# A hybrid mLSTM and retention step on one core: V of token chunk 1 for both heads in one product of 512 columns

## The chip, the core and the metric

The kernel runs on one NeuronCore of a Trainium2 chip. TensorE multiplies matrices out of SBUF into PSUM, ScalarE and VectorE read PSUM and SBUF and write SBUF, GpSimd (POOL) and SyncE help with elementwise work and issue DMAs. Each engine runs its own queue in order, and they wait for each other on semaphores. The metric is the device time of one execution in microseconds. The kernel before takes 1973.84 us (median of 3 runs, 1972.89 to 1973.92).

## The reference, cut to what matters

Two layers work on 128 context tokens and 512 latent tokens, D = 1024: layer 0 is a bidirectional mLSTM with 4 heads, layer 1 bidirectional retention with 8 heads. Each is followed by a gated feed-forward network. The part that this case is about is the projection of the tokens `u` into V, 256 columns a head:

```
def retention_mixer(u, w_in, decay_exp, g_norm, w_out, S0, grid):
    z = jnp.einsum('btd,de->bte', u, w_in).astype(F32)
    q, k, v, gate = jnp.split(z, [hk, 2 * hk, 2 * hk + hv], axis=-1)
    ...
    v = v.reshape(B, T, B_HEADS, B_DV).transpose(0, 2, 1, 3)
    ...
    h_f, S_f = retention_scan(q, k, v, log_gamma[0], S0[:, 0])
    h_b, S_b = retention_scan(flip_t(q), flip_t(k), flip_t(v), log_gamma[1], S0[:, 1])
```

The mLSTM mixer takes its q, k, v and output gate from `u @ w_in` in the same way. All is float32.

## The kernel before, in words

The 640 tokens are five chunks of 128 (`CH` = 5). Heads are worked on in pairs: two pairs in the mLSTM layer, four in the retention layer, the middle two of those in a hardware loop. For a pair, TensorE makes q, then K (two products each), then V, then for each head scores, gates, states and outputs.

Precision comes from splitting. A weight unit of 128 x 2048 numbers lands by DMA in one of four ring slots. ScalarE rounds it into `w_high[slot % 2]` (`high_unit`, L827), VectorE subtracts and gets the rest into `ring_low[slot]` (`low_unit`, L1388), and a product is the sum of three: high by high, high by low, low by high. There are only two `w_high` buffers for four slots: slot 0 (q, later gates) and slot 2 (V of the pair's first head) share the one, slot 1 (K, later gates) and slot 3 (V of the second head) the other. `high_unit(s, before)` therefore waits until the data has landed and until all products of the unit before in that buffer are made. TensorE waits in `split_unit(slot)` for VectorE's subtraction of that slot (`l_split`).

V is made chunk by chunk by `value_tile` (L2176), 24 matmuls a product (8 steps over D by 3 parts), with the tokens as the stationary operand and the weights streaming. With the weights of one head the product has 256 columns; with both (`w_high_both`, `low_both`) it has 512, one bank of PSUM. Before: chunks 0 and 1 of the first head alone, then `split_unit(3)`, chunks 2 to 4 of both heads, then chunks 0 and 1 of the second head into two banks of one slot. Two PSUM slots alternate (`pj_slot`), and ScalarE copies each product out (L975 and, for the last slot, L980). It starts the split of slot 3 before the V copies (`high_unit(3, 1)`), and that of slot 0, the gate weights, behind the copy of chunk 4 (`high_unit(0, 2)`), since w_high[0] is in use until then.

In the first pair of all, sixteen steps of a modulation product (`between(n)`, L1991, called through `after`) stand between these products. Each uses a row block of `ada_w` that is loaded two steps ahead: the DMA for step n waits for step n−2.

After V, an mLSTM pair has broadcasts of gate rows (L2282, L2283) and then the gate product (L2012); a retention pair has the scores (L2211, L2214) and then the gate product (L2012), which waits in `split_unit(0)`.

Of the kernel before, what the change touches and what calls it, by code (L numbers as in the profile page):

```python
# [9 lines left out]
ACT = mybir.ActivationFunctionType  # L10
# [10 lines left out]
CH = TOK // P  # L21
# [6 lines left out]
DK, DV = 128, 256  # L28
# [46 lines left out]
def hybrid_step(nc, x_prompt, x_sample, st_C, st_n, st_m, st_S, c_lat, c_ctx, norm_gain, ada_w, ada_b,  # L75
# [3 lines left out]
    with ExitStack() as ctx:  # L79
# [38 lines left out]
        w_high = [w_high_both[:, s, :] for s in range(2)]  # L118

        ring, ring_low = [], []  # L120
# [21 lines left out]
        vt = xflat[:, 0:vt_n].rearrange("p (c h v) -> p c h v", c=CH, h=2)  # L142
# [583 lines left out]
        def _(a):  # L726
# [208 lines left out]
            for layer in range(DEPTH):  # L935
# [13 lines left out]
                def evac_qkv(first=False, after=None, led=False):  # L949
                    if first:  # L950

                        a.wait_ge(turned, turnn.add())
                    for t in range(4):
                        out = qk[:, t, :].rearrange("p (b t) -> p b t", b=2)
                        if led and t >= 2:
                            a.wait_ge(made[1], outs[1].add())
                            a.activation(out, lead_more[t - 2], ACT.Copy, scale=DK ** -0.5).then_inc(led_out, 1)
                        else:
                            s = pj(t // 2)
                            a.activation(out, PJ[:, s, :, 0:HALF], ACT.Copy, scale=1.0 if t < 2 else DK ** -0.5  # L960
                                         ).then_inc(pj_free[s], 1)
                        if t == 1:
                            high_unit(2, 0)
                            if first:
                                gate_rows()
                    high_unit(3, 1)

                    a.wait_ge(x_saved, 16 * (layer + 1))
                    for c in range(CH):
                        s = pj(2)  # L970
                        if c < 2:
                            out, src = vt[:, c, 0, 0:DV], PJ[:, s, 0, 0:DV]
                        else:
                            out, src = vt[:, c, :, 0:DV], PJ[:, s, 0, :].rearrange("p (h v) -> p h v", h=2)
                        a.activation(out, src, ACT.Copy).then_inc(pj_free[s], 1)  # L975
                        if first and c == 2:
                            ada_row_out(P_EARLY[0])
                    high_unit(0, 2)
                    s = pj(3)
                    a.activation(vt[:, 0:2, 1, 0:DV], PJ[:, s, :, 0:DV], ACT.Copy).then_inc(pj_free[s], 1)  # L980
                    if first:
                        ada_row_out(P_EARLY[1])
                    if after:
                        after()
# [892 lines left out]
        def _(pe):  # L1877
# [13 lines left out]
            def pj_slot():  # L1891

                s = pjn.n % 2
                pjn.add()
                pe.wait_ge(pj_free[s], free[s].now())
                free[s].add()
                return s
# [212 lines left out]
            for layer in range(DEPTH):  # L2110
# [60 lines left out]
                def value_tile(out, c, high, low):  # L2171

                    for k in range(KT):
                        at = slice(k * DV, (k + 1) * DV)
                        for n, (x, w) in enumerate(((u_high, high), (u_high, low), (u_low, high))):
                            ins = pe.matmul(out, x[:, k, c * P:(c + 1) * P], w[:, :, at] if w is w_high_both or w is low_both else w[:, at],  # L2176
                                            start=(k == 0 and n == 0), stop=(k == KT - 1 and n == 2))
                    return ins

                def kv(after=None, led=False):  # L2180
                    if not led:
                        split_unit(1)
                        for m in range(2):
                            project_unit(1, m)
                            if after:
                                after(2 + m)
                    split_unit(2)
                    for c in range(2):
                        s = pj_slot()
                        value_tile(PJ[:, s, 0, 0:DV], c, w_high[0], ring_low[2]).then_inc(made[2], 1)  # L2190
                        if after:
                            after(4 + c)
                    split_unit(3)
                    for c in range(2, CH):
                        s = pj_slot()
                        value_tile(PJ[:, s, 0, :], c, w_high_both, low_both).then_inc(made[2], 1)
                        if after:
                            after(2 + 2 * c)
                            after(3 + 2 * c)
                    s = pj_slot()  # L2200
                    for c in range(2):
                        ins = value_tile(PJ[:, s, c, 0:DV], c, w_high[1], ring_low[3])
                        if c == 1:
                            ins.then_inc(made[3], 1)
                        if after:
                            after(12 + c)

                def scores(hh):

# [408 lines left out]
```

## Time and profile before

| | |
|---|---|
| median of 3 runs | 1973.84 us |
| profiled execution, own time | 1973.65 us |
| its span | 1971.9 us |
| VectorE busy | 52% |
| ScalarE busy | 35% |
| GpSimd busy | 10% |
| V products (L2176) | 1008 matmuls: 576 of 256 columns, 432 of 512 |

The page's times are of one execution, in microseconds from the span's start. PE is the stream of matmuls, PEld the loading of stationary operands beside it. Matmuls overlap, so what one costs is read from the distance between starts, or from a window over a whole product divided by its count, and not from the duration in its own row. Idle time in brackets at the end of a row of the timeline is that of the engine just before the row, with what ended it.

### The profile page before, as it was taken

The page shows a single profiled execution, that of the slowest core. Times are in us where ns is not written, and L with a number is a line of the kernel's source. Part 1 is how long each engine was busy: PE and PEld are TensorE (multiplying, and loading weights), DVE is VectorE, ACT ScalarE, POOL GpSimd, SP SyncE. Part 2 cuts the span into 40 slices and gives each one's busy share as a digit, 9 for nine tenths or more (in the row PEclk, how much of TensorE's full clock was granted, in tenths as well). Part 3 has the DMA queues.
Part 4 walks back from the last instruction along what each step waited for, and adds up shares of the span by engine and source line. Part 5 has one row for each costly group of instructions (what it writes and reads, how often), then busy time and mean ns, then how long its engine had stood idle before and what let it go on. Part 6 is the DMA issues. An engine that isn't in the chain of part 4 may idle for free.

```text
span 1971.9 us, 30380 instructions
## 1 busy us (share of the span) xinstructions
PE 1911.3 (97%) x12365; PEld 1781.4 (90%) x12365; DVE 1022.0 (52%) x1807; ACT 681.0 (35%) x872; POOL 199.5 (10%) x172
## 2 busy tenths in 40 slices
PE   7989999989999999999999999999999999999998
PEld 5758987759999999998999999998898999999997
DVE  4415446476553555568543343436377664456546
ACT  4314233344331333345322222234344332233333
POOL 4101001410000000141000000001340000000031
PEclk8989999999999999999999999999999999999999
DMA  9851202762213231344232321326742322322153
GB/s 278 315 184 61 90 28 78 256 221 65 77 54 92 76 85 51 94 139 157 70 102 70 102 64 60 111 80 215 229 107 65 86 61 67 104 67 83 34 147 116
DMA packets 270925, 218.84 MB, mean 111 GB/s; under 512 B 7995, under 2 KB 260659, under 8 KB 265203
## 3 DMA queue, kind: packets, MB, share of 16 engines
q1 hardware_dynamic: 261619, 198.96, 33.5%
q10 hardware_dynamic: 7504, 10.74, 1.6%
q0 software_dynamic: 1712, 7.88, 1.1%
q8 instruction: 64, 1.05, 0.2%
q14 instruction: 26, 0.21, 0.0%
HBM read 202.34 MB, written 11.01 MB: 108 GB/s over the span
## 4 chain that ended last, share of the span: by engine, by line
PE 83%; DVE 9%; ACT 2%; DMA 2%; issue 2%; POOL 1%; SPq 0%; DVEq 0%; ACTq 0%; POOLq 0%
PE PJ L2012 47%; PE PJ L2023 10%; PE PJ L2176 8%; PE PJ L2147 2%; PE AT L2033 2%; DVE uT L1311 1%; PE AT L2357 1%; DMA hT<-in_ada_w 1%; PE AT L1991 1%; PE AT L2373 1%; PE PJ L2033 1%; PE PJ L2493 1%; DVE diag L1298 1%; DVE xT L1307 1%; PE AT L2370 1%
## 5 line engine op out<-in xcount | busy, mean ns | idle before, releaser
L2012 PE MATMUL PJ<-h_both,w_high 128*128 128x320 f32 x3616 | 682.5, 311 | 0.3 <-DVE sq L1789 0.3
L2012 PEld LDWEIGHTS PJ<-h_both,w_high 128*128 128x128 f32 x3616 | 569.0, 188 | 3.5 <-issue 2.0
L1789 DVE SCALAR_TENSOR_TENSOR sq<-PJ,cols,sq 128x127 f32<-128x127 f32 (+2 forms) x504 | 189.0, 431 | 239.3 <-ACT sq L1153 228.2
L2012 PE MATMUL PJ<-h_both,w_low 128*128 128x320 f32 x1280 | 291.5, 309 | 0.0
L810 ACT ACTIVATE w_high<-ring 128x2048 fp32r<-128x2048 f32 (+2 forms) x92 | 159.3, 1732 | 166.4 <-PE PJ L2012 103.2
L1374 DVE TENSOR_TENSOR w_low<-ring,w_high 128x2048 fp32r<-128x2048 f32 (+2 forms) x92 | 190.9, 2075 | 45.3 <-ACT w_high L810 45.2
L2012 PEld LDWEIGHTS PJ<-h_both,w_low 128*128 128x128 f32 x1280 | 214.1, 188 | 0.0
L597 POOL TENSOR_TENSOR sqsum<-sqsum,sq 128x320 f32<-128x320 f32 x56 | 106.3, 1899 | 962.5 <-issue 804.8
L2176 PE MATMUL PJ<-w_high,h_both 128*128 128x256 f32 (+1 forms) x672 | 160.5, 330 | 0.0
L1388 DVE TENSOR_TENSOR ring_low<-ring,w_high 128x2048 fp32r<-128x2048 f32 x38 | 86.9, 2286 | 125.7 <-ACT w_high L827 124.6
L1153 ACT ACTIVATE sq<-PJ,cols 128x640 f32<-128x640 f32 x84 | 74.3, 885 | 191.7 <-PE PJ L2012 188.9
L2176 PEld LDWEIGHTS PJ<-w_high,h_both 128*128 128x128 f32 x672 | 114.5, 190 | 16.5 <-issue 5.2
L2012 PE MATMUL PJ<-h_both,ring_low 128*128 128x320 f32 x528 | 121.1, 311 | 0.0
L2176 PE MATMUL PJ<-ring_low,h_both 128*128 128x256 f32 (+1 forms) x336 | 110.4, 329 | 0.0
L2023 PE MATMUL PJ<-act_high,w_high 128*128 128x320 f32 x336 | 105.9, 315 | 1.9 <-DVE w_low L1374 1.8
L2023 PE MATMUL PJ<-act_high,w_low 128*128 128x320 f32 x336 | 103.8, 309 | 0.0
L2023 PE MATMUL PJ<-act_low,w_high 128*128 128x320 f32 x336 | 103.8, 309 | 0.0
L2012 PEld LDWEIGHTS PJ<-h_both,ring_low 128*128 128x128 f32 x528 | 89.0, 189 | 0.0
L2023 PE MATMUL PJ<-h_both,ring_low 128*128 128x320 f32 x288 | 89.0, 309 | 0.0
L2023 PE MATMUL PJ<-h_both,w_high 128*128 128x320 f32 x224 | 71.4, 319 | 2.6 <-DVE ring_low L1382 2.6
L2012 PE MATMUL PJ<-act_high,w_high 128*128 128x320 f32 x320 | 73.0, 309 | 0.0
L2012 PE MATMUL PJ<-act_low,w_high 128*128 128x320 f32 x320 | 72.9, 309 | 0.0
(288 smaller groups left out, 3037.5 us busy)
## 6 DMA issues: line engine op xcount, KB each, us to landing
ring<-in_ffn_w_up SPq DMA_DIRECT2D x88, 512.0 KB, 5.0
hT<-in_ada_w SPq DMA_DIRECT2D x30, 1024.0 KB, 5.5
ring<-in_ret_w_in SPq DMA_DIRECT2D x24, 1024.0 KB, 7.7
ring<-in_ffn_w_down SPq DMA_DIRECT2D x56, 384.0 KB, 4.1
ring<-in_ret_w_out SPq DMA_DIRECT2D x14, 1024.0 KB, 5.9
ring<-in_ml_w_in SPq DMA_DIRECT2D x12, 1024.0 KB, 9.8
turn<-in_ada_w SPq DMA_DIRECT2D x10, 1024.0 KB, 7.4
ring<-in_ffn_w_down SPq DMA_DIRECT2D x32, 320.0 KB, 3.7
```

The costliest lines, as they stand in the source:

```text
L597: pool.tensor_tensor(sum_half[:, b, :], sum_half[:, b, :], sq_y[:, n % 2, :], ALU.add).then_inc(sqy_added, 1)
L810: a.activation(w_high[s][:, 0:wide], ring[s][:, 0:wide], ACT.Copy).then_inc(h_split[s], 1)
L1153: a.activation(conv[:, b, :].rearrange("p (b t) -> p b t", b=2), src, ACT.Identity, scale=cols[:, ds(t + (COL_CONV + (layer * 3 + 1) * 2 * ...
L1298: link(v.reciprocal(rstd_half[:, b, :], rstd_half[:, b, :]))
L1374: v.tensor_tensor(w_low[s][:, 0:wide], ring[s][:, 0:wide], w_high[s][:, 0:wide].bitcast(F32), ALU.subtract).then_inc(l_split[s], 1)
L1388: v.tensor_tensor(ring_low[s][:, :], ring[s][:, :], w_high[s % 2][:, :].bitcast(F32), ALU.subtract).then_inc(l_split[s % 2], 1)
L1789: ins = v.scalar_tensor_tensor(o, z, scalar, o, ALU.mult, ALU.add)
L2012: ins = pe.matmul(PJ[:, s, b, 0:HALF], w[:, at + k * step:at + k * step + P], x[:, k, b * HALF:(b + 1) * HALF], start=(k == 0 and n == 0), ...
L2023: ins = pe.matmul(PJ[:, s, b, 0:HALF], w[:, at + k * step:at + k * step + P], x[:, k, b * HALF:(b + 1) * HALF], start=(k == 0 and n == 0), ...
L2033: ins = pe.matmul(out, w[:, at:at + P], x[:, k, b * HALF:(b + 1) * HALF], start=(k == 0 and n == 0), stop=(k == KT - 1 and n == 2))
L2147: ins = pe.matmul(PJ[:, s, b, 0:HALF], w[:, k * 256 + m * P:k * 256 + (m + 1) * P], x[:, k, b * HALF:(b + 1) * HALF], start=(k == 0 and n ...
L2176: ins = pe.matmul(out, x[:, k, c * P:(c + 1) * P], w[:, :, at] if w is w_high_both or w is low_both else w[:, at], start=(k == 0 and n == ...
```

## The change

Chunk 1 moves from the narrow products to the wide ones, for all six pairs. The first head alone is done for chunk 0 only, then `split_unit(3)` follows, then chunks 1 to 4 for both heads, then chunk 0 of the second head. ScalarE's copies follow the new shapes. The calls of `after` for the first pair are shared out anew: steps 5 and 6 behind chunk 1, 7 and 8 behind chunk 2, 9 and 10 behind chunk 3, 11 and 12 behind chunk 4, 13 behind the last product.

```
--- before.py
+++ after.py
@@ -968,7 +968,7 @@
                     for c in range(CH):
                         s = pj(2)
-                        if c < 2:
+                        if c < 1:
                             out, src = vt[:, c, 0, 0:DV], PJ[:, s, 0, 0:DV]
                         else:
                             out, src = vt[:, c, :, 0:DV], PJ[:, s, 0, :].rearrange("p (h v) -> p h v", h=2)
@@ -977,7 +977,7 @@
                     high_unit(0, 2)
                     s = pj(3)
-                    a.activation(vt[:, 0:2, 1, 0:DV], PJ[:, s, :, 0:DV], ACT.Copy).then_inc(pj_free[s], 1)
+                    a.activation(vt[:, 0, 1, 0:DV], PJ[:, s, 0, 0:DV], ACT.Copy).then_inc(pj_free[s], 1)
@@ -2185,25 +2185,22 @@
                     split_unit(2)
-                    for c in range(2):
+                    for c in range(1):
                         s = pj_slot()
                         value_tile(PJ[:, s, 0, 0:DV], c, w_high[0], ring_low[2]).then_inc(made[2], 1)
                         if after:
                             after(4 + c)
                     split_unit(3)
-                    for c in range(2, CH):
+                    for c in range(1, CH):
                         s = pj_slot()
                         value_tile(PJ[:, s, 0, :], c, w_high_both, low_both).then_inc(made[2], 1)
                         if after:
-                            after(2 + 2 * c)
                             after(3 + 2 * c)
+                            after(4 + 2 * c)
                     s = pj_slot()
-                    for c in range(2):
-                        ins = value_tile(PJ[:, s, c, 0:DV], c, w_high[1], ring_low[3])
-                        if c == 1:
-                            ins.then_inc(made[3], 1)
-                        if after:
-                            after(12 + c)
+                    value_tile(PJ[:, s, 0, 0:DV], 0, w_high[1], ring_low[3]).then_inc(made[3], 1)
+                    if after:
+                        after(13)
```

TensorE's queue in the second mLSTM pair, from the first V product to the gate product, before the change. Only each product's first row is shown; `l_split1` is the wait for VectorE's subtraction of slot 3 and `l_split0` that of slot 2 or 0, `pj_free` the wait for ScalarE's copy.

```order
L2176 MATMUL PJ<-w_high,h_both 128x256 [waits pj_free0,l_split0]
...
L2176 MATMUL PJ<-w_high,h_both 128x256 [waits pj_free1]
...
L2176 MATMUL PJ<-w_high,h_both 128x512 [waits pj_free0,l_split1]
...
L2176 MATMUL PJ<-w_high,h_both 128x512 [waits pj_free1]
...
L2176 MATMUL PJ<-w_high,h_both 128x512 [waits pj_free0]
...
L2176 MATMUL PJ<-w_high,h_both 128x256 [waits pj_free1]
...
L2282 MATMUL AT<-rM,hT 128x512 [waits h_ready]
...
L2012 MATMUL PJ<-h_both,w_high 128x320 [waits pj_free0,l_split0]
```

The same stretch with the change (the lines behind L2176 count three less):

```order
L2176 MATMUL PJ<-w_high,h_both 128x256 [waits pj_free0,l_split0]
...
L2176 MATMUL PJ<-w_high,h_both 128x512 [waits pj_free1,l_split1]
...
L2176 MATMUL PJ<-w_high,h_both 128x512 [waits pj_free0]
...
L2176 MATMUL PJ<-w_high,h_both 128x512 [waits pj_free1]
...
L2176 MATMUL PJ<-w_high,h_both 128x512 [waits pj_free0]
...
L2176 MATMUL PJ<-w_high,h_both 128x256 [waits pj_free1]
...
L2279 MATMUL AT<-rM,hT 128x512 [waits h_ready]
...
L2012 MATMUL PJ<-h_both,w_high 128x320 [waits pj_free0,l_split0]
```

The wait for `l_split1` has moved ahead by one product, and between the last wide product and the wait for `l_split0` there is one narrow product where there were two.

TensorE's queue in the very first pair, from the second V product on, before the change (L1991 is a modulation step, `early_full` its DMA):

```order
L1991 MATMUL AT<-hT,silu_c 2x512 [waits early_full0]
...
L2176 MATMUL PJ<-w_high,h_both 128x256 [waits pj_free1]
...
L1991 MATMUL AT<-hT,silu_c 2x512 [waits early_full1]
...
L2176 MATMUL PJ<-w_high,h_both 128x512 [waits pj_free0,l_split1]
...
L1991 MATMUL AT<-hT,silu_c 2x512 [waits early_full0]
...
L1991 MATMUL AT<-hT,silu_c 2x512 [waits early_full1]
```

And with the change:

```order
L1991 MATMUL AT<-hT,silu_c 2x512 [waits early_full0]
...
L2176 MATMUL PJ<-w_high,h_both 128x512 [waits pj_free1,l_split1]
...
L1991 MATMUL AT<-hT,silu_c 2x512 [waits early_full1]
...
L1991 MATMUL AT<-hT,silu_c 2x512 [waits early_full0]
...
L2176 MATMUL PJ<-w_high,h_both 128x512 [waits pj_free0]
```

Steps 5 and 6 now stand together behind chunk 1, where one product stood between them.

## Rows read from the trace of the kernel before

**Rows 1.** The page, busy time, share and instructions of each engine.
```profile
PE 1911.3 (97%) x12365; PEld 1781.4 (90%) x12365; DVE 1022.0 (52%) x1807; ACT 681.0 (35%) x872; POOL 199.5 (10%) x172
```

**Rows 2.** Windows, L2176 only: stretch, length, busy time, clock, DMA share, GB/s.
```profile
1048.52:1054.28 5.76, 5.76 (x49) 5.76 (x49) 1.00 0.60 139
1054.28:1070.62 16.34, 16.34 (x74) 13.52 (x73) 1.00 0.48 146
1070.62:1076.38 5.76, 5.76 (x49) 5.70 (x47) 1.00 0.00 0
```

**Rows 3.** Timeline, ScalarE, second retention pair: start, us, engine, line, operation.
```profile
1049.32 1.90 ACT L827 ACTIVATE w_high<-ring 128x2048 fp32r<-128x2048 f32 x1
```

**Rows 4.** Timeline, VectorE, the same stretch.
```profile
1051.26 2.29 DVE L1388 TENSOR_TENSOR ring_low<-ring,w_high 128x2048 fp32r<-128x2048 f32 x1 [12.64 <-ACT w_high L827]
```

**Rows 5.** Timeline, ScalarE, VectorE and TensorE around the gate product.
```profile
1071.32 1.91 ACT L827 ACTIVATE w_high<-ring 128x2048 fp32r<-128x2048 f32 x1
...
1073.26 2.29 DVE L1388 TENSOR_TENSOR ring_low<-ring,w_high 128x2048 fp32r<-128x2048 f32 x1 [9.81 <-ACT w_high L827]
...
1077.95 0.69 PE L2012 MATMUL PJ<-h_both,w_high 128*128 128x320 f32 x3
```

**Rows 6.** Windows, all engines: PE, PEld, DVE, ACT, POOL, clock, DMA, GB/s.
```profile
344.70:348.10 3.40, 3.40 (x8) 2.15 (x7) 3.40 (x4) 2.93 (x4) 0.00 (x0) 0.50 0.97 331
348.20:419.70 71.50, 67.27 (x440) 54.33 (x438) 41.05 (x72) 28.70 (x63) 28.54 (x23) 1.00 0.74 256
419.80:423.20 3.40, 3.34 (x9) 1.23 (x12) 3.40 (x9) 1.55 (x4) 0.00 (x0) 0.50 0.00 0
423.30:1960.00 1536.70, 1516.32 (x10010) 1462.05 (x10002) 814.19 (x1320) 527.54 (x601) 128.03 (x82) 1.00 0.32 95
```

**Rows 7.** Timeline, VectorE and TensorE, second mLSTM pair.
```profile
238.23 2.29 DVE L1388 TENSOR_TENSOR ring_low<-ring,w_high 128x2048 fp32r<-128x2048 f32 x1 [12.64 <-ACT w_high L827]
...
241.13 0.52 PE L2176 MATMUL PJ<-w_high,h_both 128*128 128x256 f32 x2
```

**Rows 8.** Timeline, TensorE, the gate product of that pair.
```profile
265.80 0.41 PE L2012 MATMUL PJ<-h_both,w_high 128*128 128x320 f32 x1
```

**Rows 9.** Timeline, VectorE and TensorE, first pair: slot 3's subtraction, modulation steps.
```profile
85.98 2.29 DVE L1388 TENSOR_TENSOR ring_low<-ring,w_high 128x2048 fp32r<-128x2048 f32 x1
...
98.93 0.61 PE L1991 MATMUL AT<-hT,silu_c 128*2 128x512 f32 x4 [1.23 <-DMA hT<-in_ada_w]
...
122.02 0.61 PE L1991 MATMUL AT<-hT,silu_c 128*2 128x512 f32 x4 [1.05 <-DMA hT<-in_ada_w]
...
126.05 0.61 PE L1991 MATMUL AT<-hT,silu_c 128*2 128x512 f32 x4
...
128.09 0.61 PE L1991 MATMUL AT<-hT,silu_c 128*2 128x512 f32 x4 [1.00 <-DMA hT<-in_ada_w]
...
132.09 0.61 PE L1991 MATMUL AT<-hT,silu_c 128*2 128x512 f32 x4 [2.96 <-DMA hT<-in_ada_w]
```

**Rows 10.** Timeline, TensorE: the other idle times of 1.8 to 2.6 us.
```profile
343.98 0.54 PE L2236 MATMUL PJ<-hT,ring 128*128 128x320 f32 x1 [2.32 <-DVE hT L1560]
...
355.59 0.41 PE L2023 MATMUL PJ<-h_both,hT_low 128*128 128x320 f32 x1 [1.82 <-ACT uT L1107]
...
419.12 0.54 PE L1936 MATMUL AT<-sq,common 128*128 128x320 f32 x1 [1.79 <-ACT sq L757]
...
434.58 0.61 PE L1991 MATMUL AT<-hT,silu_c 128*2 128x512 f32 x4 [2.17 <-DMA hT<-in_ada_w]
...
1342.99 0.48 PE L2370 MATMUL AT<-xT,diag 128*128 128x256 f32 x1 [2.56 <-DVE Sst L1692]
```

**Rows 11.** Windows, L2012 only: two gate products of 48 matmuls.
```profile
141.63:150.92 9.29, 9.29 (x48) 9.29 (x48) 0.72 0.00 0
265.80:272.86 7.06, 7.06 (x48) 7.03 (x48) 1.00 0.00 0
```

## The prediction

> **What bounds the kernel now.** I read first the table of engines: TensorE is busy for 97% of the span [rows 1], VectorE for half of it, ScalarE for a third. So the time is TensorE's stream, plus whatever TensorE waits for. Then the windows of the value products (L2176) in the second head pair of the retention layer [rows 2]. Two products of 256 columns take 5.76 us, 2.88 each, and three of 512 take 16.34, 5.45 each; the next two narrow ones take 5.76 again. Each product is 24 matmuls, so a narrow matmul costs 0.120 us and a wide one 0.227 us. A wide one does the work of two narrow ones for 0.013 less. Nothing idles in these windows. Last, the timeline of ScalarE and VectorE beside them, because the diff moves the first wide product: it reads the weights of both heads, and those of the second head have to be split by then.
>
> That split has a fixed length. ScalarE can't write w_high[1] before the K products have finished with it. It starts at 1049.32, 0.80 after TensorE went on to V at 1048.52, and takes 1.90 [rows 3]. VectorE then subtracts for 2.29 us, to 1053.55 [rows 4]. The hand-over between these two took 0.04 (1051.22 to 1051.26); for the one to TensorE I estimate 0.06 from it. So the second head's weights can be used from 1053.61, which is 5.09 us after the K products. Before, two narrow products lie in between, 5.76 us, and the wide ones start at 1054.28: a margin of 0.67 us. The change leaves one narrow product, 2.88 us.
>
> **The sum for a retention pair.** Removed: two narrow products of chunk 1, 5.76. Added: one wide one, 5.45. That alone gives 0.31 back. But the narrow product of chunk 0 ends at 1051.40 and the weights come at 1053.61: a new idle time of 2.21 us. From the new start: 1053.61 + 4 × 5.45 = 1075.41 for the end of the wide products, + 2.88 = 1078.29 for the end of V, where it was 1076.38: +1.91.
>
> Then a second wait. The gate product (L2012) that follows the scores uses w_high[0], which ScalarE may overwrite only after the last wide product. Before, that product ended at 1070.62, the split started at 1071.32 and its subtraction ended at 1075.55 (1073.26 + 2.29), 4.93 later. TensorE had 5.76 of narrow products and 1.57 of scores in between (the end of the third window of [rows 2], 1076.38, to 1077.95) and did not wait [rows 5]. Now it has 2.88 + 1.57 = 4.45, and the weights come at 1075.41 + 4.93 + 0.06 = 1080.40. The gate product starts there instead of at 1077.95: **+2.45 us** a pair, in which a wait of 0.54 stands beside the first one. The scores are on TensorE's path in either kernel. There are four such pairs (the first gets K from the code that leads into the layer, but its ScalarE and VectorE steps are the same, so I take the same chain). 4 × 2.45 = 9.8. Nothing later in a pair can take it up: from the gate product on, every chain on ScalarE, VectorE and GpSimd starts from scores or products that move along, and between 423 and 1960 us TensorE is idle only for 1.3% (20.4 of 1536.7 us in the last line of [rows 6]), mostly outside these pairs.
>
> **The mLSTM layer.** Its second pair has the same chain: the subtraction ends at 240.52 (238.23 + 2.29) and the first wide matmul, the second of the two in its row, starts at 241.25 [rows 7]. New start 240.58, so V ends 0.67 sooner at its start and 5.45 − 2.88 = 2.57 later at its end: +1.90. Behind V come 2.36 us of broadcasts (L2282) before the gate product at 265.80 [rows 8], so w_high[0] comes in time: the wide products end at 240.58 + 21.80 = 262.38, + 4.99 = 267.37, against 265.80 + 1.90 = 267.70. **+1.9**.
>
> Its first pair is interleaved with 16 modulation steps (L1991), each 1.04 us long, whose rows are loaded two ahead. The DMA of step n can start when step n−2 is done, and takes 5.0: step 12 ended at 123.06 and step 14 began at 128.09; step 13 ended at 127.09 and step 15 began at 132.09 [rows 9]. By the order, chunk 1's wide product now comes before step 5, and the last narrow one has steps 11 and 12 ahead of it and step 13 behind. Here the second head's subtraction ends at 88.27 [rows 9], after step 4 (0.4 us of wait). Step 6 waited for its DMA until 98.93 with 1.23 us idle and still does, so the longer chunk 1 (to 93.8, + 1.04 for step 5) costs nothing. From 99.97: chunk 2 105.4, steps 7 and 8 107.4, chunk 3 112.8, step 9 and the turn 114.3, step 10 115.3, chunk 4 120.8, steps 11 and 12 122.8, chunk 0 125.7, step 13 after its DMA 126.8 to 127.8, step 15 at 132.8 to 133.9, where it ended at 133.13: **+0.8**. If a DMA in there takes 1 us more it is +2; if the two loads after step 11 and 12 are quicker by as much, it is 0.
>
> **The clock.** The five new idle times of 2.2 us stand in stretches that ran at the full granted clock. What such an idle time does is in the trace. In the warm part there are six of 1.8 to 3.0 us. After 2.32 until 343.98 and after 1.79 until 419.12 the granted clock fell to half; after 1.82 until 355.59, 2.17 until 434.58 and 2.56 until 1342.99 it stayed [rows 6, 10]. The sixth, 2.96 until 132.09 [rows 9], was followed by a fall too, which still shows in the gate product at 141.63 with a mean of 0.72 [rows 11]. Three of six: so I count three falls in five (2.5, rounded up because 2.2 us lies in the middle of these lengths). The first two falls lasted 3.4 us each. Its price is from the gate product of 48 matmuls, 7.06 us at clock 1.00 and 9.29 at 0.72 [rows 11]: at 0.72 some 56% of 9.29, 5.2 us, was at half clock, and lost 2.23, so 0.43 us for each. 3.4 × 0.43 = 1.5 a fall, **+4.5** in all; the bounds are 0 and 5 × 1.5 = 7.5. The two levels are 2.4 and 1.2 GHz.
>
> The Trainium skill (TensorE: Matmul & The Clock Gate, "Why this matters for your kernels") warns only of idle gaps between bursts that are longer than these 2.2 us; by that rule no fall would come and the time would be 1986.2. The trace disagrees at 343.98 and 419.12, where shorter or equal gaps were followed by one, so this is a rival below and not the forecast.
>
> **Sum.** 9.8 + 1.9 + 0.8 + 4.5 = 17.0. The profiled execution took 1973.65 us (span 1971.9, so 1.75 around it), 0.2 below the median of 1973.84. 1973.65 + 17.0 = **1990.6 us**, 0.85% slower.
>
> The skill's figure for back-to-back matmuls (same page, "Back-to-back issue gap": N/2.4 + 2.5 ns) gives 109 ns for 256 columns and 216 for 512. By it a wide product saves nothing on two narrow ones, where the rows give 0.31; each pair would cost 0.3 more and the sum would be about 1992. The trace has 120 and 227, and goes before the page.
>
> **Rivals.**
> 1. The stalls without the falls of the clock. For it: three of the six idle times left the clock alone, and the new ones end in dense matmuls. Against it: the two in [rows 6] that did not. Time 1973.65 + 12.5 = 1986.2.
> 2. A fall after every stall, and one more where the 0.54 wait stands just before or behind the scores, whose 128-column matmuls keep the array less busy: 12.5 + 5 × 1.5 = 20.0 to 12.5 + 8 × 1.5 = 24.5, so 1993.7 to 1998. For it: 2.2 is above the shortest idle time that brought a fall. Against it: 2.56 did not bring one.
> 3. The other side: not slower, because the second head's weights are there when chunk 0 ends. The place is the split of ring slot 3, the price is then only the merge: 6 × 0.31 = 1.9 less, 1971.8 (0.1% below, no change that can be measured). It decides at 2.88 us: the chain from the end of K to the subtraction would have to be shorter than that. ScalarE's 1.90 and VectorE's 2.29 alone make 4.19, and the diff leaves them and their waits. Only if ScalarE could write w_high[1] before K is done would it hold, and the wait on the K products stands in high_unit.
> 4. The stall is there, but part is taken up later, in the first pair by the DMA (then its 0.8 is 0 or below) and in the others by the drain at the pair's end: then about half of the 12.5 is left, 1980 to 1983. For it: nothing within a pair. Against it: the idle share above.
>
> **How the numbers follow.** Measurements of this kernel can tell 0.2%, about 4 us, from no change. Chances: forecast with two to four falls (1989 to 1992.5) 0.45; rival 1, with none or one (1985.5 to 1989), 0.25; rival 2 0.15; rival 4 0.09; rival 3 0.06. The range leaves out rivals 3 and 4 and the upper part of 2: 1985 to 1995. Slower by over 0.2% is everything but rival 3 and the lowest part of 4: 0.92; within 0.2% 0.06; faster 0.02.
>
> **What would show it.** In the profile after: TensorE idle 2.2 us before the first wide matmul of L2176 with VectorE's ring_low subtraction (L1388) as the releaser, five times, and 0.4 in the first pair; idle 0.5 before the gate product in four pairs, same releaser; the wide products at 5.45 and the narrow ones at 2.88 still; V's end to V's end of the loop's pairs 2.45 longer than before; stretches of half clock beginning just behind some of the new idle times. I am wrong in the main point if the wide product starts without a wait, wrong in the second if the gate product does, and wrong in the size of the clock term if there are none or more than four new stretches at half clock. A time under 1983 would mean that something in a pair took the stall up.

## The result and the profile after

The changed kernel takes **1998.16 us** (median of 4 runs, 1996.11 to 1998.66) against 1973.75 for the kernel before (4 runs): a ratio of 1.0117, 95% interval 1.0104 to 1.0130, so 1.2% slower. The forecast was 1990.6, in a range of 1985 to 1995. The direction was right, the time lies 3 us above the range.

The profiled execution took 1996.11 us, 22.5 more than that of before. In it TensorE's waits look like this (the page of waits, the longest first: who waits for whom, us in total, times, the longest):

```profile
PE AT L1991 <- DMA hT<-in_ada_w: 11.5, 6, 3.8
PE PJ L2176 <- DVE ring_low L1388: 10.5, 6, 2.0
```

The second line is new. The value products wait six times for VectorE's subtraction, five times for 2.04 or 2.05 us and once, in the first pair, for 0.3. In the pair that [rows 2 to 5] show, ScalarE and VectorE do what they did, at the same distance from the K products (timeline of the changed kernel, ScalarE, VectorE, TensorE):

```profile
1059.23 1.90 ACT L827 ACTIVATE w_high<-ring 128x2048 fp32r<-128x2048 f32 x1
...
1061.17 2.29 DVE L1388 TENSOR_TENSOR ring_low<-ring,w_high 128x2048 fp32r<-128x2048 f32 x1 [12.64 <-ACT w_high L827]
...
1063.52 0.50 PE L2176 MATMUL PJ<-w_high,h_both 128*128 128x512 f32 x1 [2.05 <-DVE ring_low L1388]
...
1089.90 0.49 PE L2208 MATMUL AT<-uT 128*128 128x128 f32 x3
...
1092.09 0.41 PE L2012 MATMUL PJ<-h_both,w_high 128*128 128x320 f32 x1 [0.36 <-DVE ring_low L1388]
```

The subtraction ends at 1063.46 and the first wide matmul starts 0.06 later. The profile gives 2.05 us idle where I had written 2.21, since it counts from the end of the last matmul and not from where the next would have started. The last row shows the second wait, and beside it the scores (1089.90) and the gate product (1092.09) stand 2.19 apart where it was 1.57 (1076.38 to 1077.95, [rows 5]).

From V's end in this pair (1089.90) to V's end in the next (1202.77) are 112.87 us. Before, the same two were 108.65 apart (1076.38 and 1185.03), so 4.22 are added, and 2.45 of these were forecast. The rest is in the main the clock. The windows of the changed kernel, all engines, columns as in [rows 6], each 3.4 us long, with the granted clock third from the end:

```profile
98.40:101.80 3.40, 3.40 (x14) 2.17 (x7) 0.00 (x0) 0.00 (x0) 0.00 (x0) 0.51 0.68 217
...
951.80:955.20 3.40, 3.40 (x10) 2.62 (x9) 3.40 (x19) 0.00 (x0) 0.00 (x0) 0.50 0.87 235
1064.40:1067.80 3.40, 3.40 (x10) 2.63 (x9) 1.29 (x1) 0.00 (x0) 0.00 (x0) 0.50 0.87 235
1177.10:1180.50 3.40, 3.40 (x10) 2.63 (x9) 1.16 (x1) 0.00 (x0) 0.00 (x0) 0.50 0.87 230
1289.70:1293.10 3.40, 3.40 (x10) 2.61 (x9) 0.93 (x1) 0.00 (x0) 0.00 (x0) 0.50 0.88 224
```

Behind each of the four stalls in the retention layer the clock fell: TensorE ran at half clock, 1.2 instead of 2.4 GHz, beginning 0.5 to 0.9 us after it restarted. The fifth stall, at 243.47 in the mLSTM layer, brought none. The first line is in the first pair. The price of a fall can be read off directly, since in a second profile of the same kernel (the first experiment below) the stall of the first retention pair brought no fall. Windows of L2176 only, from the first V product to the start of the scores: this pair, that one without a fall, and this pair before the change.

```profile
1058.43:1089.90 31.47, 29.42 (x144) 24.93 (x144) 0.95 0.36 101
```

```profile
948.67:978.56 29.89, 27.84 (x144) 23.78 (x144) 1.00 0.38 106
```

```profile
1048.52:1076.38 27.86, 27.86 (x168) 24.98 (x168) 1.00 0.41 114
```

V takes 29.89 us without a fall of the clock and 31.47 with one, so a fall costs 1.6 us. Against 27.86 the stall alone makes V 2.03 longer, where the prediction had 1.91. The difference stands at the restart: from the first matmul behind the idle time (1063.52) to the next (1063.86) it is 0.34 us, where a wide one takes 0.227.

The first pair, TensorE's modulation steps in the changed kernel, against [rows 9]:

```profile
97.83 0.61 PE L1991 MATMUL AT<-hT,silu_c 128*2 128x512 f32 x4 [3.81 <-DMA hT<-in_ada_w]
...
107.83 0.64 PE L1991 MATMUL AT<-hT,silu_c 128*32 128x512 f32 x4 [0.72 <-ACT ada_mem L849]
...
128.80 0.61 PE L1991 MATMUL AT<-hT,silu_c 128*2 128x512 f32 x4 [0.91 <-DMA hT<-in_ada_w]
...
131.28 0.61 PE L1991 MATMUL AT<-hT,silu_c 128*2 128x512 f32 x4 [1.43 <-DMA hT<-in_ada_w]
...
134.98 0.61 PE L1991 MATMUL AT<-hT,silu_c 128*2 128x512 f32 x4 [2.67 <-DMA hT<-in_ada_w]
```

Steps 6, 8, 13, 14 and 15. The last begins at 134.98 where it began at 132.09, although this execution was about 1 us ahead when the K products of the pair ended: +2.9, or +3.9 from there. The wait of 3.81 stands where there were two, 1.23 before step 6 and 1.42 before step 7. Step 8 now waits 0.72 for a copy by ScalarE.

| part, profiled executions | forecast | measured shift |
|---|---|---|
| first pair | +0.8 | +2.9 (132.09 to 134.98) |
| second mLSTM pair | +1.9 | +2.0 |
| four retention pairs | +9.8, and most of 4.5 for the clock | +16.7, of it 4 × 1.58 = 6.3 clock |
| between the layers | 0 | +0.9 (the falls near 350 and 425 stand elsewhere) |
| sum | +17.0 with the whole 4.5 | +22.5 |

A shift is the distance of the same matmul in both traces, at the start of the part and at its end. For the retention pairs it is 5.8 us at 434.58 and 22.5 at 1295.27 (times of before). Without the clock they keep 10.4, where 9.8 was forecast: four times 2.03 for V, and four times 0.5 to 0.6 for the wait before the gate product.

The 0.9 between the layers shows that a fall did not cost the same everywhere. Before, the clock fell at 344.71, in front of TensorE's wait until 355.59, which was 1.82 us long. In the changed kernel it fell at 361.27, behind that wait, and the wait was 2.98: before, the fall was paid out of the wait, and here it was not.

### The profile page after: what moved, and what is told of

It is laid out like the page before. It is cut to its first block, busy times and chain, and to the rows that moved or that the text cites. A ratio compares the mean times of both kernels' runs of the same rounds, so it can differ in the third digit from the quotient of the medians.

```text
span 1994.3 us, 30094 instructions
## 1 busy us (share of the span) xinstructions
PE 1918.7 (96%) x12221; PEld 1778.4 (89%) x12221; DVE 1022.0 (51%) x1807; ACT 680.7 (34%) x872; POOL 199.8 (10%) x172
## 4 chain that ended last, share of the span: by engine, by line
PE 81%; DVE 10%; ACT 3%; issue 2%; DMA 2%; POOL 1%; SPq 0%; DVEq 0%; ACTq 0%; POOLq 0%
PE PJ L2012 46%; PE PJ L2023 10%; PE PJ L2176 7%; PE PJ L2147 2%; PE AT L2033 2%; DVE ring_low L1388 2%; DVE uT L1311 1%; PE AT L2354 1%; DMA hT<-in_ada_w 1%; PE AT L1991 1%; PE AT L2370 1%; PE PJ L2033 1%; PE PJ L2490 1%; ACT w_high L827 1%; DVE diag L1298 1%
## 5 line engine op out<-in xcount | busy, mean ns | idle before, releaser
L2012 PE MATMUL PJ<-h_both,w_high 128*128 128x320 f32 x3616 | 682.6, 311 | 1.6 <-DVE ring_low L1388 1.3
L2012 PEld LDWEIGHTS PJ<-h_both,w_high 128*128 128x128 f32 x3616 | 568.8, 188 | 5.7 <-issue 3.1
L2012 PE MATMUL PJ<-h_both,w_low 128*128 128x320 f32 x1280 | 291.5, 309 | 0.0
L2012 PEld LDWEIGHTS PJ<-h_both,w_low 128*128 128x128 f32 x1280 | 214.1, 188 | 0.0
L2176 PE MATMUL PJ<-w_high,h_both 128*128 128x512 f32 (+1 forms) x576 | 162.3, 367 | 10.5 <-DVE ring_low L1388 10.5
L2176 PEld LDWEIGHTS PJ<-w_high,h_both 128*128 128x128 f32 x576 | 106.5, 195 | 33.7 <-DVE ring_low L1388 12.5
L2012 PE MATMUL PJ<-h_both,ring_low 128*128 128x320 f32 x528 | 121.1, 311 | 0.0
L2176 PE MATMUL PJ<-ring_low,h_both 128*128 128x512 f32 (+1 forms) x288 | 105.1, 365 | 0.0
L2012 PEld LDWEIGHTS PJ<-h_both,ring_low 128*128 128x128 f32 x528 | 89.0, 189 | 0.0
L2012 PE MATMUL PJ<-act_high,w_high 128*128 128x320 f32 x320 | 73.0, 309 | 0.0
L2012 PE MATMUL PJ<-act_low,w_high 128*128 128x320 f32 x320 | 73.0, 309 | 0.0
```

The source lines that it names most:

```text
L2012: ins = pe.matmul(PJ[:, s, b, 0:HALF], w[:, at + k * step:at + k * step + P], x[:, k, b * HALF:(b + 1) * HALF], start=(k == 0 and n == 0), ...
```

## The experiments

**Theory A**: the time is idle time of TensorE in front of the split weights, plus half clock behind it. **Rival B**: the wide products themselves cost more. **Rival C**: the first pair costs nothing. Each experiment has its own runs of the kernel before on the same chip; where a ratio is given, it is against those.

### The changed kernel again

> The changed kernel once more, beside the others, and a second profile of it. Theory A (idle time plus clock): TensorE waits about 2.05 us for the subtraction of slot 3 in five pairs and 0.5 before the gate product in four, and most of these stalls are followed by 3.4 us at half clock, each worth 1.6 us; the number of falls differs from one execution to the next, so the time scatters by 1.6 us steps: 1996 to 1999, four to six falls behind stalls. Rival B (the wide product itself costs more, the wait is only a place where the time shows): the same time, but with the falls at other places and the wide products longer than 5.45 us.

Measured: 1997.63 us (4 runs), before 1974.19 (10 runs), ratio 1.0114 (1.0097 to 1.0130). Windows of 26 us around the stalls in the mLSTM pair and the first two retention pairs. Of the numbers only PE's busy time (26 less the stall) and the clock, 0.93 or 1.00 (third from the end), matter:

```profile
236.00:262.00 26.00, 23.95 (x119) 20.59 (x118) 2.29 (x1) 4.09 (x5) 0.00 (x0) 0.93 0.14 41
944.00:970.00 26.00, 23.95 (x128) 20.93 (x128) 18.45 (x39) 5.28 (x7) 0.12 (x1) 1.00 0.43 122
1057.00:1083.00 26.00, 23.95 (x117) 20.43 (x116) 9.08 (x4) 4.09 (x5) 2.54 (x2) 0.93 0.43 122
```

The two retention pairs that follow read 0.93 as well. Again 2.05 us idle in each and four falls of five, but not the same four: here the mLSTM stall brought one and the first retention stall none. The same code and the same idle time give either. A is confirmed in that the idle time is constant and the clock is what varies; B is out: where no fall followed, V took 29.89 us (the window above), and of that only 0.1 is neither the merge nor the stall.

### The wait alone

```
                     for c in range(2):
                         s = pj_slot()
+                        if c == 1:
+                            split_unit(3)
                         value_tile(PJ[:, s, 0, 0:DV], c, w_high[0], ring_low[2]).then_inc(made[2], 1)
...
-                    split_unit(3)
                     for c in range(2, CH):
```

> The kernel before with all products as they were, only the wait for slot 3's subtraction one product earlier, between chunks 0 and 1. Theory A: the wait alone brings nearly all: 5 x 2.2 us of idle time, 0.4 in the first pair, four or five falls of the clock of 1.6 us each; no second wait, since two narrow products still stand behind the last wide one: 1973.7 + 11.4 + 6.5 to 8 = 1991.5 to 1993. Rival B: the merge of chunk 1 is what costs, so moving the wait brings only its idle time, 1985, with no fall of the clock.

Measured: 1993.76 us (4 runs, 1993.08 to 1994.01), ratio 1.0095 (1.0078 to 1.0112). TensorE's waits:

```profile
PE PJ L2176 <- DVE ring_low L1388: 11.1, 6, 2.1
```

No product differs from the kernel before, and 19.6 of the change's 23.4 us are there, a little above the 1991.5 to 1993 that A had given. The idle time is 11.1; three of the five stalls were followed by a fall in the profile, one more came near 1362. B had 1985 and has fallen. No wait stands before the gate product here, as forecast, because two narrow products are left behind the last wide one.

### The stall filled with work

```
-                    split_unit(3)
                     for c in range(1, CH):
                         s = pj_slot()
+                        if c == 1:
+                            if not after:
+                                value_tile(PJ[:, s, 0, 0:DV], 0, w_high[0], ring_low[2], range(6))
+                            split_unit(3)
```

> The changed kernel, with 18 extra matmuls of 256 columns (six of the eight steps of chunk 0's product again, into the slot that the wide product then overwrites) put where TensorE waited in the five pairs without modulation steps. They take 18 x 0.120 = 2.16 us, as long as the wait. Theory A: the schedule is the same to 0.2 us a pair, but TensorE no longer idles, so the falls behind these stalls go: 4 to 5 x 1.6 = 6.5 to 8 us less than the changed kernel, 1990 to 1991.5. Rival B or a clock that falls for another reason: 1997 to 1999 as before, with the falls still there.

Measured: 1993.0 us (4 runs, 1989.26 to 1995.65), ratio 1.0093 (1.0075 to 1.0110). The first retention pair, the whole stretch of the four, and V of the second retention pair (L2176 only):

```profile
944.00:970.00 26.00, 26.00 (x142) 22.72 (x141) 16.87 (x39) 4.68 (x6) 0.12 (x1) 1.00 0.43 122
...
940.00:1330.00 390.00, 387.90 (x2376) 362.58 (x2376) 151.58 (x246) 105.00 (x113) 18.54 (x15) 1.00 0.27 81
...
1057.57:1087.46 29.89, 29.89 (x162) 25.94 (x162) 1.00 0.38 107
```

PE is busy for all of the 26 us and the clock stays at 1.00, in all five pairs. V takes the same 29.89 us as in the one retention pair that waited and had no fall, so the weights arrive when they did, and the 1.6 us are gone from each pair that had a fall. TensorE did useless work in that time, and that was cheaper than waiting. The runs got 4.6 us faster (1997.63 to 1993.0; the two sets scatter by 3 and 6 us), less than the 6.5 to 8 that A had. The profile has a stretch of 3.4 us at half clock near 1360 that neither profile of the changed kernel has; whether such stretches make up the rest in the other runs is not shown.

### How much must be filled

The same with six matmuls, and with three.

> As the filled kernel, but with 6 extra matmuls (0.72 us) in the stall, so that about 1.3 us of idle time are left in five pairs. If the length of a single idle time decides over the clock: no fall behind these five, since in the kernel before the idle times of 1.51 us and less near them brought none; 1990 to 1993. If any wait at this place brings a fall: three to five of them, 1996 to 1999.

> With 3 extra matmuls (0.36 us), so that about 1.7 us are left idle. If length decides and 1.79 to 1.82 us brought a fall once in two cases of the kernel before: none to three falls behind the five stalls, 1990 to 1997. If any wait at this place brings a fall: three to five.

Measured: 1990.75 us (2 runs) and 1990.59 us (2 runs); before 1974.99. The stall in the second retention pair and the clock over all four, first with six, then with three:

```profile
1061.04 0.50 PE L2176 MATMUL PJ<-w_high,h_both 128*128 128x512 f32 x1 [1.33 <-DVE ring_low L1388]
...
940.00:1330.00 390.00, 382.59 (x2326) 356.77 (x2325) 151.57 (x246) 104.73 (x113) 18.55 (x15) 1.00 0.26 80
```

```profile
1062.29 0.50 PE L2176 MATMUL PJ<-w_high,h_both 128*128 128x512 f32 x1 [1.69 <-DVE ring_low L1388]
...
940.00:1330.00 390.00, 381.15 (x2317) 355.47 (x2316) 151.57 (x246) 105.21 (x113) 18.52 (x15) 1.00 0.27 80
```

With 1.69 us left idle there was no fall behind any of the five stalls, nor with 1.33. With 2.05 to 2.14 there were 16 in 20 (the changed kernel 4 of 5, again 4, the wait alone 3, the kernel of the next section 5). So 0.36 us of work in each stall, three matmuls, were enough to keep the clock. There is one profile each at the two lengths: that 1.69 never brings a fall is not shown. Nor are the 20 cases independent of each other: in the changed kernel the stalls of the retention layer are 112.6 to 112.9 us apart and the falls behind them 112.6, so that within one profile they repeat nearly the same situation.

### The first pair as before, and the first pair alone

The two complements: the diff of the change for all pairs but the first (`alone = 2 if after else 1` for the number of narrow chunks), and for the first only.

> The changed kernel, but the first pair, with the modulation steps between its products, is as before. Theory A: the first pair's share goes, which in the profile of the changed kernel was 3.9 us: 1.6 for a fall of the clock behind a single idle time of 3.8 us, 0.72 for step 8 that now stands right behind step 7 and waits for ScalarE's copy of the row sums, the rest waits for DMAs. So 1998.0 - 3.9 = 1994 (1992.5 to 1995.5). Rival C (the first pair is hidden behind its DMAs, as I had forecast, 0.8): 1997.

> The kernel before, with only the first pair changed. Theory A: 1974.0 + 3.9 = 1977.9 (1976.5 to 1979). Rival C: 1974.8. If first_old and only_first do not add up to the whole change, the clock behind the first pair makes the difference, in steps of 1.6.

Measured: all but the first 1993.46 us (4 runs), ratio 1.0094 (1.0077 to 1.0111). The first alone 1976.57 (10 runs, 1974.0 to 1979.03), before 1974.40 (25 runs), ratio 1.0013 (1.0003 to 1.0023). So the first pair costs 2.2 by itself and 4.4 within the whole change (23.4 less 19.1, each against its own before), against my forecast of 0.8; the intervals are wide enough for the two to be the same. C has fallen by the first run, narrowly (its 1997 would be 22.6 above the kernel before, and the interval ends at 21.9), and by the shift of 2.9 in the profile. The second run alone, 0.6 to 4.5 by its interval, would allow it. A's 3.9 lies between 2.2 and 4.4. In the profile of the first alone, an execution at the low end of its runs (1974.0), step 6 waited 3.51 us, and the clock stayed up:

```profile
98.22 0.61 PE L1993 MATMUL AT<-hT,silu_c 128*2 128x512 f32 x4 [3.51 <-DMA hT<-in_ada_w]
...
97.00:101.00 4.00, 2.78 (x16) 1.61 (x17) 0.00 (x0) 0.00 (x0) 0.00 (x0) 1.00 0.90 324
```

The fall that the profile of the whole change has there is not in every execution, which is one part of the scatter.

### The first pair alone, its steps at their old chunks

```
+                            if c > 1:
+                                after(2 + 2 * c)
                             after(3 + 2 * c)
-                            after(4 + 2 * c)
...
+                        after(12)
                         after(13)
```

> The kernel before with only the first pair changed, and in it the modulation steps back at their old chunks: 5 behind chunk 1, 6 and 7 behind chunk 2, 8 and 9 behind 3, 10 and 11 behind 4, 12 and 13 behind the last product. Step 8 then no longer stands right behind step 7: its 0.72 us wait for ScalarE's copy goes. Step 6 stands behind the wide product of chunk 2 and finds its DMA landed, so the single idle time of 3.5 us and its fall of the clock go. Theory A: at least 1 us less than with the new order of steps (1976.6), so 1974 to 1976. If the first pair's cost is the longer chunk 1 itself, the same 1976.6 or more.

Measured: 1972.35 us (10 runs, 1969.61 to 1974.35), before 1974.99 (13 runs), ratio 0.9986 (0.9977 to 0.9996). That is faster than the kernel before, and 4.2 less than with the new order of steps (on another chip's runs; against each one's own before, 4.8 less). Steps 7 and 9 in its profile:

```profile
101.37 0.61 PE L1993 MATMUL AT<-hT,silu_c 128*2 128x512 f32 x4 [0.33 <-DMA hT<-in_ada_w]
...
109.31 0.61 PE L1993 MATMUL AT<-hT,silu_c 128*2 128x512 f32 x4 [0.23 <-DMA hT<-in_ada_w]
```

Step 6, at 100.00, waits for nothing. The wide product of chunk 1 is not what costs in this pair; what costs is that two steps stand behind it whose rows are not there, and that step 8 stands right behind step 7. A's direction and size hold. That the median lies 2.6 below the kernel before is more than the idle times account for (step 15 begins at 131.6 here, 132.09 before); the clock fell in other places in the profiled execution, at 124.3 and not near 345 and 420. Whether the change of the order brings that or chance did, the runs don't settle.

### Weights split in halves

The cause of the stall can be taken away: slot 3 in two halves of 1024 columns. The first wide product needs only the first for its steps 0 to 3.

```
+                a.activation(w_high[s % 2][:, 0:HU], ring[s][:, 0:HU], ACT.Copy).then_inc(h_first[s % 2], 1)
+                a.activation(w_high[s % 2][:, HU:UNIT], ring[s][:, HU:UNIT], ACT.Copy).then_inc(h_split[s % 2], 1)
...
+                    pe.wait_ge(l_first[1], firsts[1].add())
                     for c in range(1, CH):
                         s = pj_slot()
-                        value_tile(PJ[:, s, 0, :], c, w_high_both, low_both).then_inc(made[2], 1)
+                        value_tile(PJ[:, s, 0, :], c, w_high_both, low_both, (lambda: split_unit(3)) if c == 1 else None
+                                   ).then_inc(made[2], 1)
```

> The changed kernel, with slot 3 rounded and subtracted in two halves of 1024 columns and the first wide product starting on the first half (its steps 0 to 3 need no more). Theory A: first half ready 0.8 + 0.95 + 1.2 = about 2.95 us after the K products, chunk 0 takes 2.88, so the stall is under 0.2 us and its fall of the clock goes; V then ends 0.25 sooner than in the kernel before, the wait before the gate product stays at about 0.6 in four pairs. With the first pair's 3 to 4 us left: 1973.7 + 3.5 + 4 x 0.3 - 0.3 = 1978 (1976 to 1980). Rival B: the wide products cost as before, 1990 or more.

Measured: 1980.0 us (7 runs, 1978.4 to 1981.59), ratio 1.0031 (1.0019 to 1.0042). ScalarE and VectorE in the second retention pair:

```profile
1051.26 1.05 ACT L835 ACTIVATE w_high<-ring 128x1024 fp32r<-128x1024 f32 x1
1052.21 1.05 ACT L836 ACTIVATE w_high<-ring 128x1024 fp32r<-128x1024 f32 x1
...
1052.35 2.36 DVE L1402 TENSOR_TENSOR ring_low<-ring,w_high 128x1024 fp32r<-128x1024 f32 x2 [11.79 <-ACT w_high L835]
```

VectorE's two halves together take 2.36 and end at 1054.71, but the first is done by about 1053.5 (half of that time, an estimate), and the wide product starts at 1053.63 with 0.13 us idle. 17.6 of the 23.4 us are gone, and the time is the upper end of what A gave, 1976 to 1980. What was left in this profile is the wait before the gate product, and the first pair. With slot 0 in halves too:

> The changed kernel with slot 3 and slot 0 both split in halves, and the gate product starting on its first half. Theory A: the wait before the gate product, 0.28 to 0.36 in four pairs, goes: 1.2 to 1.4 less than with slot 3 alone in halves (1980.0), 1978.7. Rival D (that wait is not the split but the scores' drain): unchanged, 1980.

Measured: 1978.68 us (10 runs, 1974.16 to 1981.68), ratio 1.0020 (1.0010 to 1.0029). The four waits are gone from the profile: the gate product starts 1.58 us after the scores in each of the four pairs, where it was 2.1 to 2.2 with slot 3 alone in halves, which makes 2.3 us. The medians are 1.3 apart, as A had it, though that is less than the scatter of these runs. Rival D (the drain of the scores) has fallen by the profile.

### Towards a faster kernel

> Halves for slots 3 and 0, and the first pair as before: no stall of the change is left and the five later pairs have 24 wide matmuls in place of 48 narrow ones. Theory A: 1974.0 - 5 x 0.31 = 1972.4 (1971.5 to 1974), if the halves themselves cost TensorE nothing. Rival B (wide products cost more than their rows show): 1975 or more.

Measured (halves for both slots, first pair as before): 1976.77 us (10 runs, 1973.27 to 1978.24), before 1974.40, ratio 1.0004 (0.9995 to 1.0014). Not the 0.999 that was expected, and by its number rival B's case (1975 or more); no difference to the kernel before can be told. The profile, of an execution of 1977.8, has no wait of the change left but shows, between 50 and 1950 us, 13.6 us more at half clock than that of before (new stretches near 100, 438 and 1346, and one near 131 that is 3.4 longer), none of which stands behind a stall of the change. It also shows that the merge brings nothing here. V of the second retention pair in it:

```profile
1051.19:1079.16 27.97, 27.84 (x144) 23.78 (x144) 1.00 0.40 113
```

That is 0.1 longer than the 27.86 before, not 0.31 shorter. The timeline of the kernel with slot 3 in halves shows why (the first row joins the last narrow matmul, 1053.22, and the first wide one, which the second row shows by itself):

```profile
1053.22 0.91 PE L2200 MATMUL PJ<-w_high,h_both 128*128 128x256 f32 x2
...
1053.63 0.50 PE L2200 MATMUL PJ<-w_high,h_both 128*128 128x512 f32 x1
1053.97 0.40 PE L2200 MATMUL PJ<-ring_low,h_both 128*128 128x512 f32 x1
```

Behind 1053.22 the next matmul could start at 1053.34. The wide one starts 0.29 later, and the one behind it 0.34 after that instead of 0.227. The two together, 0.4, are more than the 0.31 of the merge, though the idle time in the profile reads 0.13. It is not the wide products that cost more, as rival B had it, but the way into them.

> Chunk 1 wide in all six pairs, slots 3 and 0 split in halves (no stall in the five later pairs), and the first pair with its modulation steps at their old chunks. Theory A: the 1972.4 of the first pair alone (2.2 to 2.6 below the kernel before on the same chip) less 5 x 0.31 = 1.5 in the later pairs: 3.5 to 4 below the kernel before, ratio 0.998. Rival E (the 2.6 of the first pair alone came from the places where the clock fell by chance in those executions): 1.9 below, ratio 0.999. Rival B: at or above the kernel before.

Measured (halves for both slots, all six pairs, steps at their old chunks): 1974.64 us (11 runs, 1971.54 to 1977.16), before 1975.35 (15 runs), ratio 0.9992 (0.9983 to 1.0001). Rival E's 1.9 us below fit (the interval goes from 3.4 below to 0.2 above), the 3.5 to 4 of theory A don't, and the 0.31 in each of the five later pairs, which both sums contain, is not there, as just shown. The time alone doesn't exclude rival B (at or above the kernel before) either. It is 1.2% faster than the change as made (0.9992 against 1.0114), and against the kernel before no difference can be told, since the interval holds 1.

## Why the prediction was wrong in size

In the profiled execution 22.5 us were added where the sum had 17.0. Of the 5.5 between them 2.1 are in the first pair, 1.8 are the clock behind the stalls (6.3 for 4.5), 0.9 stand between the layers, and 0.6 and 0.1 are in the retention pairs (the restart and the second wait) and in the second mLSTM pair. The median lies 2 us above this execution; the second profile, of 1997.35 us, has 6.8 us more at half clock between 50 and 1950 us, which is argued as the reason and not shown for each run.

- **The split's chain and the first wait: right.** The wide products started 0.06 behind the subtraction, at the forecast distance from K, in five pairs, and 5.45 and 2.88 stood. The merge gave its 0.31 back, but 0.1 of it went at the restart: V grew by 2.03 where 1.91 was forecast.
- **The second wait: right.** Scores to gate product grew by 0.5 in the first and 0.6 in the second retention pair, 0.54 forecast; it vanished with slot 0 in halves.
- **The clock term: the step that failed by its size.** I had three falls of 1.5 for five stalls, 4.5. Both profiles of the changed kernel have four behind the stalls, at 1.6 each, 6.3, and one more in the first pair, which is five new stretches at half clock where more than four was my sign of being wrong in this term. Over the four profiles with stalls of this length it is 16 in 20. I took the share, three in six, from idle times that differ in what stands around them: only one of the six, 1.82 until 355.59, lay between dense products, and it was shorter than 2.05. So the case that mattered was not in the sample. The price, 1.5 against 1.6, I took from a product of 320 columns whose share at half clock was worked out from a mean; the number of falls was the larger error. The Trainium skill's warning (TensorE: Matmul & The Clock Gate, "Why this matters for your kernels") names longer gaps only. The traces disagree: here gaps of 2.05 to 2.14 us were followed by a fall in 16 of 20 cases.
- **The first pair: the other step that failed.** 0.8 was forecast; the profile has 2.9 (3.9 from the K products), the runs 2.2 and 4.4. The step reads "Step 6 waited for its DMA until 98.93 with 1.23 us idle and still does, so the longer chunk 1 (to 93.8, + 1.04 for step 5) costs nothing". The wait's end was right (97.83, 1 us ahead as all of that execution), but its beginning moved: the idle time became 3.81, and a fall of the clock came with it (1.6 in the step and the product behind it). I also read the order and overlooked that step 8 begins a new sum, `ada_row`, and so waits for ScalarE's copy behind step 7: 0.72. In the kernel before, a product stood between them.
- **Rivals.** Rival 2 (five to eight falls, 1993.7 to 1998) came nearest, and had 0.15. Its number is close in part by luck: no fall stood at the wait before the gate product, and not every stall had one; the first pair made up for these. Rivals 1, 3 and 4 were wrong: nothing took the stalls up.

## What to carry to other kernels

A product that is merged to save streaming time needs all of its operands at its start. Count the time from the moment the shared buffer is free to the moment the last converted operand is there, and keep that much other work in front; here 5.1 us against 2.9. A wait in a dense stream of matmuls was paid twice here, once as idle time and most times once more as half clock behind it, and converting in two pieces took away nearly all of both. But even the short wait that was left cost 0.4 us where the profile shows 0.13 idle, more than the merge saves: compare the length of the whole stage, and not only the idle time. Where a step waits for a DMA, watch the length of its wait and not only its end.

## What the runs showed of the hardware

Idle times of 2.05 to 2.14 us in a dense stream were followed by 3.4 us at 1.2 GHz in 16 of 20 cases (four profiles), and each such stretch cost 1.6 us (V 31.47 against 29.89); with 1.69, 1.33 or no idle time in the same place there was none in 15 (three profiles). Whether a given execution has the fall is not decided by the code: the same kernel had it behind different stalls in two profiles, and once a wait of 3.51 us passed without. The first wide matmul behind such an idle time took 0.34 us to the next one, and not 0.227. The executions of one kernel scatter by up to 8 us (the kernel before from 1971.33 to 1978.89 in 25 runs), which up to five falls more or less would make; that they do is argued from the profiles, and not shown for each run.
